# Two transformer blocks on one core: the second block's products set between the mLSTM steps, inputs laid out by the host, products of ones at the start, and 8 KB pieces in the experts' and feed-forward tiles

## The reference, cut to what matters

```python
def first_block(x, mem, ...):
    h = x
    for layer in range(2):
        h = h + hybrid_mixer(rmsnorm(h, norm_mix_g[layer]), ...)
        h = h + memory_cross_attention(rmsnorm(h, norm_x_g[layer]), rmsnorm(mem, norm_mem_g[layer]), ...)
        hn = rmsnorm(h, norm_ffn_g[layer])
        if layer == 0:
            h = h + swiglu(hn, ffn_w_gate, ffn_w_up, ffn_w_down)         # width 2816
        else:
            h = h + moe_swiglu(hn, moe_router, moe_w_gate, ...)          # 8 experts of width 3584, top 2
    return rmsnorm(h, norm_final_g)

def second_block(x, ...):
    h = rms_norm(x, norm1_g)
    xm, o_pre, gate_pre, xl, lru_gate, merge_pre = split(h @ w_in)
    y_m = mlstm_branch(xm, o_pre, gate_pre, ...)      # 4 heads, forward and backward, rms norm per head
    y_l = lru_branch(xl, lru_gate, ...)               # conv of 4 taps, block gates r and i, scan both ways
    g_m, g_l = split(sigmoid(merge_pre))
    merged = g_m * (y_m @ w_branch_mlstm) + g_l * (y_l @ w_branch_lru)
    x = x + merged @ w_out
    x = x + peer(rms_norm(x, norm2_g), ...)           # 8 heads x 16 rows per token out of 16384
    return rms_norm(x, final_norm_g)
```

## Time and profile before

| what | value |
|---|---|
| median of 3 runs | 2906.54 us |
| the profiled execution's own time | 2900.36 us |
| its span, first to last instruction | 2898.3 us |
| TensorE busy (matmul) | 2676.4 us, 92% |
| VectorE, ScalarE, GpSimd busy | 1883.5, 1086.2, 247.0 us |
| mean granted TensorE clock | 0.965 of full |
| DMA | 775.16 MB, mean 267 GB/s |

### The profile page before, as it was taken

How to read it: one execution, slowest core, us unless ns; L and a number is a source line. 1 busy time by engine, 2 the same in 40 slices (tenths; PEclk the granted TensorE clock), 3 DMA queues, 4 the chain that set the end, 5 groups by cost and what they waited for, 6 DMA issues and landing times.

```text
span 2898.3 us, 31279 instructions
## 1 busy us (share of the span) xinstructions
PE 2676.4 (92%) x11630; PEld 2044.6 (71%) x11630; DVE 1883.5 (65%) x2833; ACT 1086.2 (37%) x1145; POOL 247.0 (9%) x280
## 2 busy tenths in 40 slices
PE   8999999999899999999999999788999998777777
PEld 7768899868778888888888888677888443333332
DVE  5331653631388889897888888254443877887875
ACT  2112332121276768677776866121231111110110
POOL 0000000000000000000000000000001344334331
PEclk9999999999899999999999999899999999989999
DMA  6330653521289999999999997441354999999997
GB/s 217 133 116 29 204 189 133 192 101 58 102 293 333 371 336 362 341 353 349 332 373 333 352 353 282 152 154 44 102 189 161 386 421 421 421 421 422 422 421 322
DMA packets 280203, 775.16 MB, mean 267 GB/s; under 512 B 13786, under 2 KB 55464, under 8 KB 247336
## 3 DMA queue, kind: packets, MB, share of 16 engines
q1 hardware_dynamic: 241284, 503.54, 48.8%
q0 software_dynamic: 36864, 268.45, 22.4%
q10 hardware_dynamic: 1956, 1.86, 0.2%
HBM read 772.76 MB, written 1.05 MB: 267 GB/s over the span
## 4 chain that ended last, share of the span: by engine, by line
PE 78%; DMA 12%; DVE 7%; ACT 1%; issue 1%; DVEq 0%; ACTq 0%
PE banks L533 14%; PE banks L694 13%; PE banks L696 13%; PE banks L695 13%; DMA dense_weights<-in_peer_rows,work 11%; PE banks L581 5%; PE banks L1060 5%; PE banks L657 2%; PE banks L661 2%; PE banks L494 2%; PE banks L1022 1%; PE banks L851 1%; DVE dense_weights L2295 1%; PE banks L780 1%; PE banks L807 1%
## 5 line engine op out<-in xcount | busy, mean ns | idle before, releaser
L1977 DVE TENSOR_TENSOR expert_tiles_low<-expert_tiles,expert_tiles_high 128x2048 fp32r<-128x2048 f32 x336 | 753.0, 2287 | 89.8 <-ACT expert_tiles_high L1505 89.7
L1505 ACT ACTIVATE expert_tiles_high<-expert_tiles 128x2048 fp32r<-128x2048 f32 x336 | 624.8, 1912 | 65.8 <-DMA expert_tiles<-in_moe_w_down 53.0
L1060 PE MATMUL banks<-dense_weights,work 128*128 128x512 f32 x952 | 461.9, 638 | 113.8 <-DVE work L2305 113.6
L1060 PEld LDWEIGHTS banks<-dense_weights,work 128*128 128x128 f32 x952 | 188.5, 204 | 377.1 <-issue 212.5
L694 PE MATMUL banks<-expert_tiles_high,gathered_parts 128*128 128x512 f32 x896 | 355.4, 397 | 2.2 <-DVE gathered_parts L1986 2.2
L696 PE MATMUL banks<-expert_tiles_high,gathered_parts 128*128 128x512 f32 x896 | 350.5, 391 | 0.0
L695 PE MATMUL banks<-expert_tiles_low,gathered_parts 128*128 128x512 f32 x896 | 349.8, 390 | 0.0
L2295 DVE CUSTOM_DVE_ANT_0 dense_weights<-dense_weights,banks 128x1024 f32<-128x1024 f32 x238 | 286.3, 1219 | 86.6 <-DMA dense_weights<-in_peer_rows,work 84.5
L1313 POOL DMA_INDIRECT dense_weights<-in_peer_rows,work x238 | 223.9, 941 | 741.9 <-DVE work L2267 382.2
L1682 ACT ACTIVATE work<-work 128x2 f32<-128x2 f32 x129 | 26.2, 203 | 560.8 <-DVE work L2295 560.4
L533 PE MATMUL banks<-normed,dense_weights 128*128 128x256 f32 x1024 | 225.7, 383 | 5.9 <-DVE normed L1721 5.9
(11 more groups left out here) (355 smaller groups left out, 3526.8 us busy)
## 6 DMA issues: line engine op xcount, KB each, us to landing
expert_tiles<-in_moe_w_gate SPq DMA_DIRECT2D x112, 1024.0 KB, 5.1
expert_tiles<-in_moe_w_up SPq DMA_DIRECT2D x112, 1024.0 KB, 5.2
expert_tiles<-in_moe_w_down SPq DMA_DIRECT2D x112, 1024.0 KB, 4.9
dense_weights<-in_w_in SPq DMA_DIRECT2D x12, 2048.0 KB, 8.0
dense_weights<-in_w_xkv SPq DMA_DIRECT2D x8, 2048.0 KB, 8.1
dense_weights<-in_w_in SPq DMA_DIRECT2D x10, 1280.0 KB, 13.8
expert_tiles<-in_ffn_w_gate SPq DMA_DIRECT2D x11, 1024.0 KB, 5.3
expert_tiles<-in_ffn_w_up SPq DMA_DIRECT2D x11, 1024.0 KB, 5.4
```

What stands on the lines that cost most here:

```text
L1060: mm = pe.matmul(halves[half], diag[(first + j) % 8], pair_row(first + j)[:, 1, half * 512:(half + 1) * 512], start=False, stop=end and j ...
L1505: act.activation(high_tile(j), raw_tile(j), ACT.Copy).then_inc(g.high, 1)
L1977: dve.tensor_tensor(low_tile(j), raw_tile(j), high_tile(j).bitcast(F32), ALU.subtract).then_inc(g.split, 1)
```

## The change

1. The host lays out `x`, `mem`, the spatial weights, the router and all parameter vectors as they will lie on chip. `x` is loaded straight into `hF`, `mem` into `mem_hat`, the spatial weights into `spatialT`, and the vectors as one matrix into `cols`. The 50 transposes of the first layer and their copies go. Of the small loads 4 are left, on ScalarE's queue. SyncE issues `x` and then the first weights.
2. TensorE runs 13 products of `ones` with `ones` before anything else. ScalarE takes their bank before it squares.
3. In the 8 mLSTM steps TensorE runs one group (16 matmuls) of xl (steps 0 to 3) or merge_m (steps 4 to 7) ahead of the wait for `intra`. ScalarE copies them out. The sigmoid of merge_m is made later, in place. VectorE does one tap of xl's convolution in each of steps 4 to 7.
4. Behind the steps: two groups of gate r, the head norm, the rest of r and i of direction 0, gate_l, the gates of direction 1, then branch_m. VectorE multiplies branch_m into `merged` after the LRU. SyncE's loads follow the same order, and five buffers move to other places.
5. Expert and feed-forward tiles are stored on the host so that each partition's 8 KB of a tile are contiguous.
6. `peer()` gets a padding transpose where a count of banks is odd (one on the "v" side here).

```diff
+            pe.wait_ge(ones_ready, 1)
+            bank = G.begin("a", "warm")
+            for _ in range(WARM):
+                mm = pe.matmul(bank[:, 0:P], ones[:, :], ones[:, :], start=True, stop=True)
+            G.end(mm)
             pe.wait_ge(consts_ready, 1)
...
-            features_first("v", "x", x_in)
             norm_sums(("mix_ms", 0))
             pe.wait_ge(params_loaded, 16 * N_PARAMS)
...
-                if l == 0:
-                    memory()
...
+                merge_m, xl = linear_groups("merge_m", "a", 2, x), linear_groups("xl", "a", 2, x)
                 for i in range(2 * HEADS):
...
                         maxima(i + 1)
+                    next(xl if i < HEADS else merge_m)
                     pe.wait_ge(intra_ready, i + 1)
...
-                linear("merge_m", "a", 2, x, KT)
+            def lru_gates(d, names, groups):
+
+                pe.wait_ge(xl_conv_ready, 1)
+                for name in names:
...
             def lru():
                 x = lambda k: xF[:, k, :]
-                linear("xl", "a", 2, x, KT)
+                gate_slots["r"], gate_slots["i"] = G.tile(), G.tile()
+                gates_at = len(G.freed)
+                lru_gates(0, ("r",), (0, 1))
+                head_norm()
+                lru_gates(0, ("r",), (2, 3))
+                lru_gates(0, ("i",), range(4))
+                linear("gate_l", "a", 2, x, KT)
+                lru_gates(1, ("r", "i"), range(4))
+                G.freed[gates_at - 2] = G.freed[gates_at - 1] = (group_done, G.total)
                 pe.wait_ge(ym_ready, 1)
                 linear("branch_m", "v", 2, lambda k: hM[:, k, :], KT)
...
+                    if i >= HEADS:
+                        tap = i - HEADS
+                        dve.wait_ge(act_took, G.took["xl", 3])
+                        conv(xl_conv, lambda k, j: xl_pad[:, k, j:j + SEQ], tap + 1, ...)
...
-            sp.dma_start(x_in, t["x"].rearrange("o (b p) d -> p (o b) d", p=P)).then_inc(x_loaded, 16)
-            more_layer_params(sp)
-            last_params(sp)
+            sp.dma_start(hF[:, :, :], t["x"]).then_inc(x_loaded, 16)
...
-                        src = (gate, up)[j // 2 % 2][:, bass.ds(e * KT + half * (KT // 2), KT // 2), c * 512:(c + 1) * 512]
+                        src = (gate, up)[j // 2 % 2][:, bass.ds(e * 2 * CHUNKS + 2 * c + half, 1), :]
...
+                    for dst, src in square_parts():
+                        act.wait_ge(x_loaded, 16)
+                        act.activation(dst, src, ACT.Square).then_inc(sq_ready, 1)
...
+                ready(("num", 2 * HEADS - 1))
+                lru_gate("r", 0, (0, 1))
                 act.wait_ge(h_sum_ready, 1)
                 square(hM)
```

More of the change, by code:

```diff
@@ L538, in linear, with linear_groups @@
                     G.free()
+            def linear_groups(key, who, n_tiles, x):
+                for tile in range(n_tiles):
+                    slot = G.tile()
+                    w = weight(slot, KT, None)
+                    for g in range(2):
+                        bank = G.begin(who, (key, 2 * tile + g))
+                        for i in range(2):
+                            for k in range(KT):
+                                mm = pe.matmul(bank[:, i * SEQ:(i + 1) * SEQ], w[:, k, (2 * g + i) * P:(2 * g + i + 1) * P], x(k),
+                                               start=(k == 0), stop=(k == KT - 1))
+                        G.end(mm, (key, 2 * tile + g))
+                        if g == 1:
+                            G.free()
+                        yield
             def weight(slot, kts, widths, cols_n=None):
@@ L961, in mlstm, with head_norm @@
                     G.end(mm)
-                linear("merge_m", "a", 2, x, KT)
+            def lru_gates(d, names, groups):
+                pe.wait_ge(xl_conv_ready, 1)
+                for name in names:
+                    w = ring[:, gate_slots[name], 0:16 * P].rearrange("p (k n) -> p k n", k=16)
+                    for g in groups:
+                        bank = G.begin("a", (name, d, g))
+                        for i in range(2):
+                            mm = pe.matmul(bank[:, i * SEQ:(i + 1) * SEQ], w[:, 8 * d + 2 * g + i, :], xl_conv[:, 2 * g + i, :],
+                                           start=True, stop=True)
+                        G.end(mm)
+            def head_norm():
                 pe.wait_ge(sq_ready, seen.next("sq"))
@@ L1127, in more_layer_params @@
[L1127 to L1142, removed]
-            param(queue, rows[LC_W:LC_W + 32, 4, :], t["lru_conv_w_2"][0].rearrange("j (k c) -> (j k) c", c=P))
-            vec(queue, FIN_G, 4, t["norm_final_g"])
-            param(queue, router[:, :, :], t["moe_router"][0].rearrange("(k p) e -> p k e", p=P))
@@ L1269, in _ @@
             step = Steps(pool, pool_step)
+            pool.memset(ones[:, :], 1.0).then_inc(ones_ready, 1)
             step.then(pool.memset(ident[:, :], 0.0))
@@ L1691, in peer @@
                         share(u + AHEAD_UNITS)
+                    elif part == 1 and u == PHEADS - 2 and G.pad_a:
+                        ready("pad_a")
+                        take(act.activation(final_std[:, 0:1], banks_of("pad_a")[:, 0:1], ACT.Copy))
                     if n == BLOCK_BATCHES + LATE:
@@ L1731, in add_to_residual, with conv @@
                     take(dve.tensor_tensor(s, pair(bank_of((key, g))), s, ALU.add))
-            def conv(dst, src, taps, weight, bias, tiles):
-                for j in range(taps):
+            def conv(dst, src, taps, weight, bias, tiles, first=0):
+                for j in range(first, taps):
                     for k, m in tiles:
@@ L1746, in conv @@
                 step.settle()
[L1748 to L1754 removed]
+            dve.wait_ge(x_loaded, 16)
+            dve.wait_ge(params_loaded, 16 * N_PARAMS)
             def memory():
[L1758 removed]
+                dve.wait_ge(memory_loaded, 32)
                 dve.memset(spatialT[64:P, :, :, 0:64], 0.0).then_inc(mask_ready, 1)
@@ L2123, in argument @@
                     ins.then_inc(arg_ready, 1)
+                step.then(dve.memset(xl_pad[:, :, 0:2], 0.0))
+                step.then(dve.memset(xl_pad[:, :, 2 + SEQ:], 0.0))
+                step.settle()
                 argument(0)
@@ L2205, in lru @@
                 dve.tensor_tensor(h_l, h_l, gate_l, ALU.mult).then_inc(yl_ready, 1)
+                dve.wait_ge(merge_gate_ready, 1)
+                for g in range(4):
+                    ready(("branch_m", g))
+                    take(dve.tensor_tensor(merged[:, 2 * g:2 * g + 2, :], pair(bank_of(("branch_m", g))), g_m[:, 2 * g:2 * g + 2, :], ALU.mult))
             def merge():
```

221 lines of the change are left out of this document (105 added, 116 removed).

## The result

| | before | after |
|---|---|---|
| median of 5 runs | 2902.61 us | 2888.13 us |
| lowest and highest | 2895.82, 2906.89 | 2884.15, 2892.52 |
| ratio, 95% interval | | 0.9948 [0.9929, 0.9968] |
| profiled execution, span | 2900.36, 2898.3 us | 2885.73, 2884.0 us |
| mean granted clock | 0.965 | 0.967 |

The change saves 14.5 us by the medians and 15.1 by the ratio. The forecast was 22.1 us saved and a time of 2884.4. The time looks closer (3.7 us off) than the saving (7 us off), because two more runs of the kernel before moved its median from 2906.5 to 2902.6. The question is where 7 us went.

What follows compares the result with a forecast made beforehand. TensorE's chain of float32 matmuls was taken as the bound until the gathers take over at 2290 us. Savings of 7.4 (start) and 14.7 (mLSTM part) make 22.1 us: median 2906.5 to 2884.4, range 2877 to 2896.

Steps and rivals of the forecast that it cites:

- The step that failed: At the gathers: the padding transpose is one short instruction beside VectorE's work, costing below 0.3 us.
- the last stage as long as before: Sign of being right: the last stage, where the gathers take over, keeps its length.
- The start: Up to the first mixer products: 3.2 for an earlier first product, 2.8 for transposes, 1.4 for clock; 7.4 us saved.
- of the clock: Early mixer products: half of the 2.85 us lost at the lower clock is saved, 1.4 us, bounds 0 and 2.85.
- the ones: Before the sums: products meant to raise the clock; forecast to gain nothing, since the sums already ran at full rate.
- The mLSTM part: From step 0 to the end of w_out: 251.4 us against 266.1, 14.7 us saved, bounds 9 and 17.
- The steps: The 8 mLSTM steps: 85.7 us of TensorE work if it never waits; VectorE keeps up with a microsecond to spare.
- the first rival: mLSTM part: groups do not fit under VectorE's round, or gates wait for tables and low clock; 2891 to 2901, 14%.
- The tail: From gate_l through direction 1 gates, branch_m, merge_l and branch_l to the end of w_out: 146.9 us.
- Behind the steps: From last numerators through head norm and direction 0 gates: 16.3 us plus 2.5 for clock in two pauses, 18.8.
- The tiles: Expert loop: 8 KB tiles gain nothing, since TensorE does not wait for tiles; any gain bounded by 6.7 us.
- The gathers: Last stage: 256 x 1 MB of rows at the same rate in the same buffers, only beginning earlier.

Runs made afterwards that it cites:

- Run 4: Changed kernel with the padding transpose and VectorE's read of it moved ahead of w_out; ratio 0.9928 to the kernel before, 20.9 us saved.
- run 1: Changed kernel with mLSTM steps, LRU and tiles as before, leaving the new start and padding transposes; ratio 0.9993 to the kernel before, 2.0 us saved.
- run 2: Kernel before with only the reordered mLSTM and LRU part, no padding transpose; ratio 0.9958 to the kernel before, 12.2 us saved.
- Run 5: Run 4 with one gate_l group put ahead of the head norm, then all direction 0 gates; ratio 0.9894 to the kernel before, median 2872.0 us.
- run 6: Changed kernel with the head norm ahead of all direction 0 gate groups; ratio 0.9932 to the kernel before, 19.8 us saved.
- run 3: Kernel before with only the contiguous 8 KB expert and feed-forward tiles; ratio 1.0002 to the kernel before, 0.6 us lost.
- run 7: Changed kernel with one product of ones at the start instead of 13; ratio 0.9939 to the kernel before, 17.7 us saved.
- run 8: Changed kernel with 14 identity transposes at the start instead of 13 products of ones; ratio 0.9943 to the kernel before, 16.6 us saved.

## Why the prediction was right and wrong

**The step that failed** is one sentence: "The padding transpose is one short instruction beside VectorE's work, below 0.3 us." The instruction is short: 0.27 us on TensorE, 0.15 on VectorE. What it costs is its bank. It measured 5.9 us in the changed kernel, 3.9 of later start and 2.0 of lower clock. Run 4, which moves it and nothing else, gives 5.8 us more than the changed kernel by the ratios. Their intervals overlap, so this rests on the stretch behind w_out, 691.9 us against 699.1. Runs 1 and 2 show that the loss comes with the padding and not with the steps. The prediction costed the instruction, and did not ask in which order its reader takes it. Of its signs of being right, "the last stage as long as before" is the one that failed. The code also has a place for a padding group on ScalarE's banks; the trace has neither its transpose nor its copy, so it played no part.

**The start**, 7.4 forecast, 7.0 to 7.2 measured, by its terms: first product 3.0 earlier (3.2 forecast), transposes 2.84, and of the clock 1.2 (1.4 forecast). The last is read from the 144 records: 23.77 and 10.59 for the 48 behind the transposes, 34.36 us before, 33.15 after, 31.46 at full rate. That 1.4 and 1.2 agree is luck: 1.4 was half of an all-or-nothing loss of 2.85, and in runs 1, 5 and 6 the whole 2.9 is saved. x landed after 5.49 us instead of 5.16. The Trainium skill (DMA: Bandwidth & Descriptors, "Issuing engines are not separate DMA queues") says that loads of all issuing engines interleave, and the prediction made up to 0.8 us of it for the parameters. The direction agrees, the cause is not shown: x also has another layout now, and the first weights are issued at 1.27 us, right behind it, where before they were at 8.56.

A right number with a wrong reason is the ones. I took the sums' 3.46 us behind transposes as proof that transposes raise the clock. The same start ran the same sums in 3.63 us in run 2 and in 4.30 in run 3: the row was one execution's, at the kind end. The term stood only because the loss moves: an earlier first product met the lower clock, a later one did not.

**The mLSTM part**, 14.7 forecast, 13.1 measured. The steps take 85.2 us (85.7 forecast), with TensorE busy 77.99 us by modelled ends in the 81 us between 1939 and 2020 (3.0 of them the first pause) and no wait for VectorE's decay matrix: the convolution taps fit, and the first rival had no part. The tail takes 146.8 (146.9). Behind the steps it was 21.0 instead of 18.8, and that term was mis-sized twice. The second pause is 3.9, not 2.7: I hid ScalarE's table load of 1.28 us under TensorE's work, but it stands ahead of the first sigmoid, between VectorE's signal and the squares (2021.44 in the chain above). And the clock took 3.3 in the head norm, not 2.5. In runs 2, 7 and 8, with the same order, this part took 21.7 to 21.8 us: in all three the two gate groups between the pauses were slow too (3.75 us where it was 1.97), and the second pause was 3.1. Run 5 shows that this is the right list: it removes the pauses and the lower clock and gets 9.0 of 10.5.

**The tiles**: nothing, as forecast, within 3 us. **The gathers**: begun earlier and as long as before (from the end of the first query product to the end of the span 679.7 us, before 679.6), right in itself. Their start is where the 5.9 us came in.

The sum as measured: 7.2 + 13.1 - 5.9 = 14.4, against 14.3 by the spans. As single changes against before the parts give 2.0 + 12.2 - 0.6 = 13.6, so within these intervals they neither help nor hinder each other.

## What to carry to other kernels

When a change adds a group to a rotation of banks, cost the whole rotation, not the instruction: which later group inherits the bank, who must read it, and what stands ahead of that read. A filler belongs where its reader is idle. When a pause can't be removed, put work into it that is due anyway; this gave 9.0 us, and shortening it 3.4. And compare the same stretch in several executions before one row of it is taken as a rule: here the sums of one start took 3.46, 3.63 and 4.30 us.

## What was not expected of the hardware

The granted clock can take back what an early start wins. In the five kernels with 13 products of ones and the new start the first mixer product began at 13.78, 13.87, 14.17, 14.28 and 14.42 us. The first two met the lower clock (33.15 us for 144 records), the last three did not (31.46). The later start has a visible cause: in the first two the products of ones took 4.7 and 4.9 us, in the last three 5.5 to 5.7. In those three the ones, not x, released ScalarE's squares, which began at 6.6 to 6.9 us instead of 6.3. So the start at 13.87 was 0.3 us ahead of that at 14.17 and 1.4 us behind it at mem's sums (47.02 and 45.63). And a single pause of 5.26 us (run 6) brought less of the lower clock, 2.0 us, than two pauses of 3.3 and 3.9 with two gate groups between them, 3.3 us. What decides this between pauses of the same length was not found.

Executions also differ by as much as the loss that this document explains. From mem's sums to the first scores, work that no run changes but for the tiles, the profiles of runs 3 and 6 took 1888.0 us and the other eight 1880.9 to 1883.9. That is why the stages are compared here, and not only the times.
